# Reordering the three partial products inside whole matmul units of an encoder step on one Trainium2 core

## The chip, the cores and the metric

One core of one Trainium2 chip. The metric is the device time of one execution in microseconds, as the median of the runs; the profile is one further execution, recorded by the hardware profiler. Engines are TensorE (PE; its weight loads are PEld), VectorE (DVE), ScalarE (ACT), GpSimd (POOL) and SyncE (SP), which issues most DMAs.

## What is computed

A two-layer encoder trunk for 512 prompt positions and 64 sample positions, which share all weights. Cut to what matters:

```python
for i in range(2):
    h = x + 0.5 * rmsnorm(swiglu(rmsnorm(x), f1_up, f1_down))     # FFN 1, 1024 -> 2 x 2816 -> 1024
    u = rmsnorm(h)
    branch inputs, gates = split(u @ w_in)                         # 1024 -> 2816 + 4096
    y_n = branch_n(...) @ w_branch[n]                              # conv, gated recurrence, two attentions
    m = sum_n sigmoid(gate_n) * y_n
    h = h + rmsnorm(m @ w_out)
    h = h + 0.5 * rmsnorm(swiglu(rmsnorm(h), f2_up, f2_down))     # FFN 2
    h = h + rmsnorm((p[i] @ ple_w) * sigmoid(rmsnorm(h) @ ple_gate_w))
```

All data are float32. The kernel works with activations turned, features on the 128 partitions and all T = 576 positions along the free axis.

## The kernel before, in words

**Three products.** Each float32 operand is held as a rounded part and a remainder (`whi`/`wlo` for weights, `u_hi`/`u_lo`, `s_hi`/`s_lo`, `o_hi`/`o_lo`, `m_split[..0]`/`m_split[..1]` for inputs). A product is rounded weights by rounded inputs, plus rounded weights by input remainders, plus weight remainders by rounded inputs, all added up in PSUM.

**Units.** A unit is one load of weights of 128 x 1024 (128 output features, up to 8 input tiles of 128), 512 KB by one DMA into one of RAW = 4 slots of `wraw`. A unit yields 128 output features for all 576 positions, in two halves of 288. So a whole unit is 8 tiles x 3 products x 2 halves = 48 matmuls. The third unit of each down-projection output has 6 tiles. A layer has 222 units: 44 + 24 for FFN 1, 22 projections, 40 of gates and branches, 8 of the output projection, 44 + 24 for FFN 2, 2 + 8 for the per-layer embedding (PLE).

**How a unit's weights come.** SyncE loads into slot i % 4 when `w_split` says that the slot's last user is split (`load_unit`, L505). ScalarE rounds `wraw` into `whi[i % 2]` when unit i - 2 is done (`act_round`, L499 to L503) and counts `w_rounded`. GpSimd then makes `wlo[i % 2]` (L1830 to L1832) and counts `w_split`. TensorE waits on `w_split` at the start of the unit (`split_ready`, L541).

**How TensorE walks a unit.** `products` (L527 to L539) goes by input tile k; per tile it runs all three products, six matmuls. `wait_k` waits ahead of each tile, in the units whose inputs are still being made: the first after a norm, and the first output-projection unit. Line L536 is the matmul of all units.

**Norm and first unit.** After a norm's sum (`pe_norm_y` L572, `pe_norm_h` L581) TensorE broadcasts the factors into PSUM (`pe_broadcast` L565) and runs filler matmuls (`keep_clock` L549): 14 calls ahead of FFN 1, 6 calls ahead of the others. Then VectorE makes the eight normed tiles `uf[k]` (L742), ScalarE rounds each to `u_hi[k]` (L659, signal `u_high`), and the remainder `u_lo[k]` is made by GpSimd for k = 1, 2, 4, 5, 6 and by VectorE for k = 0, 3, 7 (`low`, L736; signals `u_ready_pool` and `u_ready`). `u_tile_ready` (L589) waits for the remainder of tile k. There are four such first units in a layer: FFN 1, projections, FFN 2, PLE gate.

**Gated sum and output projection.** `dve_gates` (L1577) makes the gated sum tile by tile: it adds up `msum`, casts it into `m_split[:, m, 0]` (L1596), makes the remainder (L1597) and counts `m_ready`. `pe_out` (L1546) runs the eight output-projection units; the first waits for `m_ready` tile by tile.

**Partial units.** Where a unit is laid between steps of a recurrence or an attention, `unit_part` (L809) runs two or three tiles of it at a time through `products`; the branch products in `pe_gates` (L1523) use `products` too.

Of the kernel before, what the change touches and what calls it, by code (L numbers as in the profile page):

```python
# [33 lines left out]
HT = T // 2  # L34
# [10 lines left out]
KD = D // 128  # L45
# [15 lines left out]
U_UP, U_DOWN = 2 * KF, 3 * KD  # L61
U_FFN = U_UP + U_DOWN
U0_FFN1 = 0
U0_PROJ = U_FFN
U0_GATE = U0_PROJ + NPROJ
# [7 lines left out]
SPLIT = 2  # L73
# [15 lines left out]
def trunk(nc, a, o):  # L89
    n_consts = [0]  # L90
    n_placed = [0]
    with ExitStack() as ctx:
# [26 lines left out]
        whi = keep("whi", [SPLIT, 1024], F32R)  # L119
# [407 lines left out]
        def products(pe, part, x_hi, x_lo, ks, k_off, p, start, stop, wait_k=None):  # L527

            ins = None
            for n, k in enumerate(ks):  # L530
                if wait_k is not None:
                    wait_k(k)
                w = slice(128 * (k_off + n), 128 * (k_off + n) + 128)
                for c, (wt, x) in enumerate(((whi, x_hi), (whi, x_lo), (wlo, x_hi))):
                    for f in range(2):
                        ins = pe.matmul(ps[:, 2 * p + f, 0:HT], wt[:, part, w], x[:, k, HT * f:HT * f + HT],  # L536
                                        start=start and n == 0 and c == 0, stop=stop and n == len(ks) - 1 and c == 2,
                                        skip_group_check=True)
            return ins  # L539

        def split_ready(pe, i):  # L541
            pe.wait_ge(w_split, i + 1 + RAW)

# [45 lines left out]
        def u_tile_ready(pe, n):  # L589

            def wait(k):
                if k in LO_POOL:
                    pe.wait_ge(u_ready_pool, len(LO_POOL) * (n // 2) + LO_POOL.index(k) + 1)
                else:
                    pe.wait_ge(u_ready, len(LO_DVE) * (n // 2) + LO_DVE.index(k) + 1)
            return wait

        def pe_ffn(pe, f, u0):
            if f == 0:
                keep_clock(pe, 14)  # L600
                pe_norm_y(pe, N_F1PRE)
            else:
                pe_norm_h(pe, N_F2PRE)
            with pe.Fori(0, KF // 2) as it:
                for q in range(4):
                    i = it * 4 + (u0 + q)
                    split_ready(pe, i)

                    pe.wait_ge(up_mul, it * 2 + (f * KF + q // 2 + 1))

                    products(pe, (u0 + q) % SPLIT, u_hi, u_lo, range(KD), 0, q, True, True,
                             wait_k=u_tile_ready(pe, 4 * f + N_F1PRE) if q == 0 else None).then_inc(unit_done, 1)
            with pe.Fori(0, 2) as it:
                for m in range(4):
                    for q, (k0, k1) in enumerate(DOWN_K):
                        i = it * 12 + (u0 + U_UP + 3 * m + q)
                        split_ready(pe, i)
                        if q == 0:

                            pe.wait_ge(y_ready, it * 4 + (m + 1 + y_before[4 * f + N_F1POST]))  # L620
                        if m == 0 and q != 1:

                            pe.wait_ge(s_ready, f * KF + 2 + (KF - 1 if q == 0 else KF))
                        products(pe, (u0 + U_UP + 3 * m + q) % SPLIT, s_hi, s_lo, range(k0, k1), 0, m, q == 0, q == 2).then_inc(unit_done, 1)
            if f:
                pe_turn_p(pe)
            pe.wait_ge(y_ready, 4 + y_before[4 * f + N_F1POST] + 5)
            pe_norm_y(pe, 4 * f + N_F1POST)
# [186 lines left out]

        def pe_proj_free(pe, t):

            split_ready(pe, U0_PROJ + t)
            if t >= 2:
                pe.wait_ge(proj_out, t - 1)  # L820

        def pe_proj(pe, t):
            i = U0_PROJ + t
            pe_proj_free(pe, t)
            products(pe, i % SPLIT, u_hi, u_lo, range(KD), 0, t % 2, True, True,
                     wait_k=u_tile_ready(pe, N_MPRE) if t == 0 else None).then_inc(unit_done, 1)

        def pe_proj_part(pe, t, j, parts):
            if j == 0:
                pe_proj_free(pe, t)  # L830
            unit_part(pe, U0_PROJ + t, j, t % 2, parts)

# [253 lines left out]

        def pe_gate_free(pe, g):

            split_ready(pe, U0_GATE + g)
            if g == 0:  # L1090
                pe.wait_ge(proj_out, NPROJ)
            elif g < GATES_CONV:
                pe.wait_ge(gate_out, g - 1)
            else:
                pe.wait_ge(gate_out, g)

        def pe_kept_gate(pe, g):
            pe_gate_free(pe, g)
            products(pe, (U0_GATE + g) % SPLIT, u_hi, u_lo, range(KD), 0, g % 2, True, True).then_inc(unit_done, 1)

        def pe_gate_part(pe, n, last, step, parts):

            g, j = n + step // len(parts), step % len(parts)
            if g < last:
                if j == 0:
                    pe_gate_free(pe, g)
                unit_part(pe, U0_GATE + g, j, 0, parts)

# [414 lines left out]
        def pe_gates(pe):  # L1523
            with pe.Fori(0, 2) as it:
                for m in range(4):
                    u0 = U0_PAIR + 3 * m
                    i = it * 12 + u0
                    split_ready(pe, i)
                    if m == 0:
                        pe.wait_ge(gate_out, 2 * KD)  # L1530
                    for n in range(NB):
                        if m == 0:
                            pe.wait_ge(o_ready, 2 * n + 2)
                        if n >= 2:

                            pe.wait_ge(sig_done, it * 8 + (2 * m + n - 1))
                        ins = products(pe, u0 % SPLIT, o_hi, o_lo, (2 * n, 2 * n + 1), 2 * n, n, True, True)
                    ins.then_inc(unit_done, 1)
                    for n in (2, 3):
                        split_ready(pe, i + (n - 1))  # L1540
                        pe.wait_ge(yb_out, it * 16 + (4 * m + n - 1))
                        products(pe, (u0 + n - 1) % SPLIT, u_hi, u_lo, range(KD), 0, n, True, True).then_inc(unit_done, 1)

                    pe.wait_ge(yb_out, it * 16 + (4 * m + 4))

        def pe_out(pe):  # L1546
            for m in range(KD):
                i = U0_OUT + m
                split_ready(pe, i)
                if m >= 4:  # L1550
                    pe.wait_ge(y_ready, y_before[N_MPOST] + m + 1)

                products(pe, i % SPLIT, m_split[:, :, 0, :], m_split[:, :, 1, :], range(KD), 0, m % 4, True, True,
                         wait_k=(lambda k: pe.wait_ge(m_ready, k + 1)) if m == 0 else None).then_inc(unit_done, 1)
            pe.wait_ge(y_ready, 4 + y_before[N_MPOST] + 5)
            pe_norm_y(pe, N_MPOST)

# [129 lines left out]
        def pe_ple(pe):  # L1687
            for q in range(2):
                i = U0_PLEW + q
                split_ready(pe, i)  # L1690
                pe.wait_ge(p_ready, 2)
                for m in range(4):

                    j = 4 * q + m
                    if j >= 3:
                        pe.wait_ge(e_out, j - 2)
                    for kk in range(2):
                        for c, (wt, x) in enumerate(((whi, p_hi), (whi, p_lo), (wlo, p_hi))):
                            for f in range(2):
                                ins = pe.matmul(ps[:, 2 * (j % 3) + f, 0:HT], wt[:, i % SPLIT, 512 * kk + 128 * m:512 * kk + 128 * m + 128],  # L1700
                                                x[:, kk, HT * f:HT * f + HT], start=kk == 0 and c == 0, stop=kk == 1 and c == 2, skip_group_check=True)
                    ins.then_inc(e_made, 1)
                pe.wait_ge(e_made, 4 * q + 4)
                pe.sem_inc(unit_done, 1)
            pe.wait_ge(e_out, KD)
            pe_norm_h(pe, N_PPRE)
            for m in range(KD):
                i = U0_PLEG + m
                split_ready(pe, i)
                if m >= 4:  # L1710
                    pe.wait_ge(ple_sig, m - 3)
                products(pe, i % SPLIT, u_hi, u_lo, range(KD), 0, m % 4, True, True,
                         wait_k=u_tile_ready(pe, N_PPRE) if m == 0 else None).then_inc(unit_done, 1)
            pe.wait_ge(ple_sig, 5)
            pe_norm_y(pe, N_PPOST)

# [253 lines left out]
```

## Time and profile before

| | |
|---|---|
| median of 3 runs | 3511.64 us (3510.53 to 3516.72) |
| profiled execution, its own time | 3519.2 us |
| span of its instructions | 3517.5 us |
| TensorE matmuls busy | 3266.0 us, 23523 matmuls |
| weight loads busy | 3105.9 us |
| VectorE, ScalarE, GpSimd busy | 1386.8, 1096.2, 1206.1 us |
| mean granted clock of TensorE | 0.957 |
| moved by DMA | 236.25 MB, mean 67 GB/s |

The busy time of an engine is the time in which at least one of its instructions runs. A matmul's row lasts about 0.29 us since matmuls overlap; what a matmul costs is the distance from one start to the next. A wait is told as "engine, line waited for <- engine and line that released it". A granted clock of 1.00 is 2.4 GHz, 0.50 is 1.2 GHz.

### The profile page before, as it was taken

How to read it: one execution, taken by the hardware profiler on the slowest of the kernel's cores; microseconds unless marked ns; L12 is line 12 of the kernel's file. 1: busy time of each engine (PE TensorE's matmuls, PEld its weight loads, DVE VectorE, ACT ScalarE, POOL GpSimd, SP SyncE). 2: the span in 40 equal slices, each digit the busy share in tenths (PEclk: the TensorE clock that was granted, in tenths of full speed). 3: DMA queues.
4: the chain of work that ended last, by engine and by line, in shares of the span. 5: the costliest groups of instructions: out<-in, count | busy, mean ns of one | idle time of the engine just before them, and what ended most of it. 6: DMA issues, size and time to landing. Idle time of an engine off the chain costs nothing. (4 is left out here: it accounts for less than half of the span.)

```text
span 3517.5 us, 56480 instructions
## 1 busy us (share of the span) xinstructions
PE 3266.0 (93%) x23523; PEld 3105.9 (88%) x23523; DVE 1386.8 (39%) x1793; ACT 1096.2 (31%) x1518; POOL 1206.1 (34%) x538
## 2 busy tenths in 40 slices
PE   8999998877999999999889999988789999999997
PEld 7999986776699899999789999867676998999987
DVE  4222144784444323312333321548844433332133
ACT  3332231124533333323233322311255333333232
POOL 4333442131134433344333334411211434333442
PEclk9999998998999999999899999989899999999988
DMA  3222211121122122232022222111210221222211
GB/s 95 83 81 82 83 57 49 37 77 51 31 66 78 55 83 78 82 89 75 13 85 82 79 84 83 54 41 44 67 53 26 78 82 56 82 79 87 83 59 40
DMA packets 455963, 236.25 MB, mean 67 GB/s; under 512 B 18630, under 2 KB 454150, under 8 KB 455814
## 3 DMA queue, kind: packets, MB, share of 16 engines
q1 hardware_dynamic: 445792, 227.05, 22.1%
q10 hardware_dynamic: 10022, 7.15, 0.7%
q8 instruction: 102, 1.67, 0.2%
q14 instruction: 47, 0.39, 0.0%
HBM read 228.53 MB, written 5.63 MB: 67 GB/s over the span
## 5 line engine op out<-in xcount | busy, mean ns | idle before, releaser
L1832 POOL TENSOR_TENSOR wlo<-wraw,whi 128x1024 fp32r<-128x1024 f32 x432 | 1076.3, 2492 | 2122.3 <-ACT whi L503 2122.3
L536 PE MATMUL ps<-u_hi,whi 128*128 128x288 f32 x4800 | 1062.2, 302 | 36.3 <-ACT ybr L1565 11.8
L536 PE MATMUL ps<-u_lo,whi 128*128 128x288 f32 x4800 | 1038.2, 297 | 0.0
L536 PE MATMUL ps<-u_hi,wlo 128*128 128x288 f32 x4800 | 1037.2, 297 | 0.0
L536 PEld LDWEIGHTS ps<-u_hi,whi 128*128 128x128 f32 x4800 | 778.4, 191 | 73.3 <-issue 33.0
L536 PEld LDWEIGHTS ps<-u_lo,whi 128*128 128x128 f32 x4800 | 779.5, 190 | 0.0
L536 PEld LDWEIGHTS ps<-u_hi,wlo 128*128 128x128 f32 x4800 | 778.0, 190 | 0.0
L503 ACT ACTIVATE whi<-wraw 128x1024 fp32r<-128x1024 f32 x432 | 456.9, 1058 | 959.0 <-PE ps L536 958.5
L783 DVE TENSOR_TENSOR sq<-sq,ps 128x576 f32<-128x576 f32 x88 | 66.4, 754 | 751.0 <-PE ps L536 751.0
L536 PE MATMUL ps<-s_hi,wlo 128*128 128x288 f32 x1408 | 302.7, 296 | 0.0
L536 PE MATMUL ps<-s_lo,whi 128*128 128x288 f32 x1408 | 302.7, 296 | 0.0
L536 PE MATMUL ps<-s_hi,whi 128*128 128x288 f32 x1408 | 302.6, 296 | 0.0
L720 DVE TENSOR_TENSOR sqsum<-sqsum,sq 128x576 f32<-128x576 f32 x70 | 102.0, 1458 | 506.5 <-ACT sq L638 504.3
L787 DVE TENSOR_TENSOR s_lo<-sq,s_hi 128x576 f32 x88 | 241.5, 2745 | 10.9
L536 PEld LDWEIGHTS ps<-s_hi,whi 128*128 128x128 f32 x1408 | 226.5, 189 | 0.0
L536 PEld LDWEIGHTS ps<-s_hi,wlo 128*128 128x128 f32 x1408 | 226.5, 189 | 0.0
L536 PEld LDWEIGHTS ps<-s_lo,whi 128*128 128x128 f32 x1408 | 226.3, 189 | 0.0
L1167 DVE SCALAR_TENSOR_TENSOR yc<-zc,taps,yc 128x606 f32<-128x606 f32 x120 | 134.4, 1122 | 4.2
L503 ACT ACT_TABLE_LOAD x44 | 56.5, 1283 | 232.4 <-PE ps L536 232.4
L553 PE MATMUL ps<-ident,ones 128*128 128x128 f32 x528 | 88.3, 333 | 22.9 <-issue 18.7
L553 PEld LDWEIGHTS ps<-ident,ones 128*128 128x128 f32 x528 | 82.7, 244 | 23.3 <-issue 23.2
L854 ACT ACTIVATE proj<-ps 128x576 f32<-128x576 f32 x28 | 18.3, 652 | 233.6 <-PE ps L536 233.6
(277 smaller groups left out, 2985.3 us busy)
## 6 DMA issues: line engine op xcount, KB each, us to landing
wraw<-in_ffn_up SPq DMA_DIRECT2D x176, 512.0 KB, 3.8
wraw<-in_w_in SPq DMA_DIRECT2D x104, 512.0 KB, 3.8
wraw<-in_ffn_down SPq DMA_DIRECT2D x64, 512.0 KB, 3.8
wraw<-in_ffn_down SPq DMA_DIRECT2D x32, 384.0 KB, 3.3
wraw<-in_w_out SPq DMA_DIRECT2D x16, 512.0 KB, 3.8
wraw<-in_ple_gate_w SPq DMA_DIRECT2D x16, 512.0 KB, 3.8
wraw<-in_w_branch SPq DMA_DIRECT2D x16, 256.0 KB, 2.7
xtok<-in_x_prompt SPq DMA_DIRECT2D x4, 512.0 KB, 6.6
```

The costliest lines, as they stand in the source:

```text
L503: act.activation(whi[:, i % SPLIT, :], wraw[:, i % RAW, :], ACT.Copy).then_inc(w_rounded, 1)
L536: ins = pe.matmul(ps[:, 2 * p + f, 0:HT], wt[:, part, w], x[:, k, HT * f:HT * f + HT], start=start and n == 0 and c == 0, stop=stop and n ...
L553: pe.matmul(ps[:, 1, 0:128], ones[:], ident[:], start=True, stop=True)
L720: dve.tensor_tensor(sqsum[:], sqsum[:], sq[:, k % 2, :], ALU.add).then_inc(sq_added, 1)
L783: dve.tensor_tensor(halves(x), halves(x), pair(2 * q + 1), ALU.mult).then_inc(up_mul, 1)
L787: dve.tensor_tensor(s_lo[:, bass.ds(it * 2 + q, 1), :].rearrange("p a n -> p (a n)"), x, s_hi[:, bass.ds(it * 2 + q, 1), :].rearrange("p a ...
L854: ins = act.activation(x, y_, ACT.Copy, scale=HD ** -0.5 if t in (BQ_, BQ_ + 1) else 1.0)
L1167: ins = dve.scalar_tensor_tensor(out=yc[:, c, :], in0=zc[:, c, w:w + YW], scalar=wc, in1=yc[:, c, :], op0=ALU.mult, op1=ALU.add)
L1832: pool.tensor_tensor(wlo[:, i % SPLIT, :], wraw[:, i % RAW, :], whi[:, i % SPLIT, :], ALU.subtract).then_inc(w_split, 1)
```

## The change

`products` stays for partial units. Whole units (FFN up and down, whole projections, kept gates, the gates in `pe_gates`, output projection, PLE gate) go through a new function `unit`. It runs one product over all tiles of the unit, then the next: rounded weights by rounded inputs, rounded weights by input remainders, weight remainders by rounded inputs. The wait for `w_split` moves to the start of the last third; at the start of the unit stands a wait for `w_rounded`. In the first units after a norm the first third waits for `u_high` tile by tile and the second third for the remainders as before. In the first output-projection unit the first third waits for `m_ready`. Partial units call `split_ready` themselves, ahead of their first part.

```diff
+        def unit(pe, i, part, x_hi, x_lo, ks, p, start, stop, wait_hi=None, wait_k=None):
+            pe.wait_ge(w_rounded, i + 1)
+            ins = None
+            for c, (wt, x) in enumerate(((whi, x_hi), (whi, x_lo), (wlo, x_hi))):
+                if c == 2:
+                    split_ready(pe, i)
+                for n, k in enumerate(ks):
+                    if c == 0 and wait_hi is not None:
+                        wait_hi(k)
+                    if c == 1 and wait_k is not None:
+                        wait_k(k)
+                    w = slice(128 * n, 128 * n + 128)
+                    for f in range(2):
+                        ins = pe.matmul(ps[:, 2 * p + f, 0:HT], wt[:, part, w], x[:, k, HT * f:HT * f + HT],
+                                        start=start and n == 0 and c == 0, stop=stop and n == len(ks) - 1 and c == 2,
+                                        skip_group_check=True)
+            return ins
...
+        def u_high_ready(pe, n):
+            return lambda k: pe.wait_ge(u_high, 8 * (n // 2) + k + 1)
...
-                    split_ready(pe, i)
                     pe.wait_ge(up_mul, it * 2 + (f * KF + q // 2 + 1))
-                    products(pe, (u0 + q) % SPLIT, u_hi, u_lo, range(KD), 0, q, True, True,
-                             wait_k=u_tile_ready(pe, 4 * f + N_F1PRE) if q == 0 else None).then_inc(unit_done, 1)
+                    unit(pe, i, (u0 + q) % SPLIT, u_hi, u_lo, range(KD), q, True, True,
+                         wait_hi=u_high_ready(pe, 4 * f + N_F1PRE) if q == 0 else None,
+                         wait_k=u_tile_ready(pe, 4 * f + N_F1PRE) if q == 0 else None).then_inc(unit_done, 1)
...
-                split_ready(pe, i)
                 if m >= 4:
                     pe.wait_ge(y_ready, y_before[N_MPOST] + m + 1)
-                products(pe, i % SPLIT, m_split[:, :, 0, :], m_split[:, :, 1, :], range(KD), 0, m % 4, True, True,
-                         wait_k=(lambda k: pe.wait_ge(m_ready, k + 1)) if m == 0 else None).then_inc(unit_done, 1)
+                unit(pe, i, i % SPLIT, m_split[:, :, 0, :], m_split[:, :, 1, :], range(KD), m % 4, True, True,
+                     wait_hi=(lambda k: pe.wait_ge(m_ready, k + 1)) if m == 0 else None).then_inc(unit_done, 1)
```

The down-projection units, the whole projections, the kept gates, the two gate units in `pe_gates` and the PLE gate units are changed in the same way; counted over both layers, 388 units go through `unit`.

## Rows read from the trace of the kernel before

**Rows 1.** The page, busy time of each engine.
```profile
PE 3266.0 (93%) x23523; PEld 3105.9 (88%) x23523; DVE 1386.8 (39%) x1793; ACT 1096.2 (31%) x1518; POOL 1206.1 (34%) x538
```

**Rows 2.** TensorE's waits: waiter <- releaser, us in total, times, longest us.
```profile
PE ps L536 <- POOL u_lo L736: 11.6, 28, 0.6
...
PE ps L536 <- DVE u_lo L736: 5.7, 6, 1.1
...
PE ps L536 <- POOL wlo L1832: 1.5, 2, 0.8
...
PE ps L536 <- DVE m_split L1597: 0.3, 2, 0.2
```

**Rows 3.** FFN 1's up-projections: stretch, us; busy PE, PEld, DVE, ACT, POOL; clock, DMA, GB/s.
```profile
52.00:320.00 268.00, 268.00 (x2012) 268.00 (x2011) 83.15 (x63) 85.07 (x85) 104.20 (x42) 1.00 0.28 81
```

**Rows 4.** Timeline of FFN 2's first unit: start, us, engine, line, operation, xcount [idle <- releaser].
```profile
1209.20 1.56 PE L553 MATMUL ps<-ident,ones 128*128 128x128 f32 x12
1211.87 0.51 PE L536 MATMUL ps<-u_hi,whi 128*128 128x288 f32 x2 [1.11 <-DVE u_lo L736]
...
1219.66 0.53 PE L536 MATMUL ps<-u_hi,whi 128*128 128x288 f32 x2 [0.32 <-POOL u_lo L736]
1220.03 0.42 PE L536 MATMUL ps<-u_lo,whi 128*128 128x288 f32 x2
...
1221.35 0.43 PE L536 MATMUL ps<-u_hi,whi 128*128 128x288 f32 x2
...
1210.25 1.41 ACT L659 ACTIVATE u_hi<-uf 128x576 fp32r<-128x576 f32 x2 [3.42 <-DVE uf L742]
1212.49 2.13 ACT L659 ACTIVATE u_hi<-uf 128x576 fp32r<-128x576 f32 x3 [0.82 <-DVE uf L742]
1216.04 2.13 ACT L659 ACTIVATE u_hi<-uf 128x576 fp32r<-128x576 f32 x3 [1.42 <-DVE uf L742]
...
1218.21 2.02 DVE L736 TENSOR_TENSOR u_lo<-uf,u_hi 128x576 fp32r<-128x576 f32 x1 [0.75 <-ACT u_hi L659]
...
1216.80 2.80 POOL L736 TENSOR_TENSOR u_lo<-uf,u_hi 128x576 fp32r<-128x576 f32 x2 [0.23 <-ACT u_hi L659]
```

**Rows 5.** Timeline of the first output-projection unit, first layer.
```profile
1133.53 0.70 PE L536 MATMUL ps<-m_split,whi 128*128 128x288 f32 x4
...
1136.08 2.53 DVE L1596 CAST m_split<-msum 128x576 fp32r<-128x576 f32 x1
...
1138.64 0.76 DVE L1597 TENSOR_TENSOR m_split<-msum,m_split 128x576 fp32r<-128x576 f32 x1
...
1139.45 0.79 PE L536 MATMUL ps<-m_split,whi 128*128 128x288 f32 x4 [0.15 <-DVE m_split L1597]
...
1140.35 0.70 PE L536 MATMUL ps<-m_split,whi 128*128 128x288 f32 x4
```

**Rows 6.** TensorE's clock: stretch, us, busy PE, clock, DMA, GB/s; below, the sums at 1186.85.
```profile
551.60:554.60 3.00, 0.01 (x1) 0.94 0.35 67
...
556.40:561.40 5.00, 4.97 (x16) 0.54 0.48 105
...
1186.20:1189.10 2.90, 2.06 (x17) 1.00 0.24 73
...
1190.60:1195.90 5.30, 5.26 (x18) 0.50 0.35 99
...
1211.90:1221.40 9.50, 7.79 (x49) 1.00 0.00 0
...
970.00:974.10 4.10, 3.81 (x16) 0.50 0.00 0
...
1186.85 1.27 PE L559 MATMUL ps<-ones,sqsum 128*128 128x1 f32 x10 [0.64 <-DVE sqsum L720]
```

**Rows 7.** Timeline at half clock: two matmuls in each row, first branch product.
```profile
971.87 0.69 PE L536 MATMUL ps<-o_hi,whi 128*128 128x288 f32 x2
972.35 0.69 PE L536 MATMUL ps<-o_lo,whi 128*128 128x288 f32 x2
```

More of the change, by code:

```diff
@@ L623, in pe_ffn @@
                             pe.wait_ge(s_ready, f * KF + 2 + (KF - 1 if q == 0 else KF))
-                        products(pe, (u0 + U_UP + 3 * m + q) % SPLIT, s_hi, s_lo, range(k0, k1), 0, m, q == 0, q == 2).then_inc(unit_done, 1)
+                        unit(pe, i, (u0 + U_UP + 3 * m + q) % SPLIT, s_hi, s_lo, range(k0, k1), m, q == 0, q == 2).then_inc(unit_done, 1)
             if f:
@@ L816, in pe_proj_free @@
         def pe_proj_free(pe, t):
-            split_ready(pe, U0_PROJ + t)
             if t >= 2:
@@ L824, in pe_proj @@
             pe_proj_free(pe, t)
-            products(pe, i % SPLIT, u_hi, u_lo, range(KD), 0, t % 2, True, True,
-                     wait_k=u_tile_ready(pe, N_MPRE) if t == 0 else None).then_inc(unit_done, 1)
+            unit(pe, i, i % SPLIT, u_hi, u_lo, range(KD), t % 2, True, True,
+                 wait_hi=u_high_ready(pe, N_MPRE) if t == 0 else None, wait_k=u_tile_ready(pe, N_MPRE) if t == 0 else None).then_inc(unit_done, 1)
         def pe_proj_part(pe, t, j, parts):
             if j == 0:
+                split_ready(pe, U0_PROJ + t)
                 pe_proj_free(pe, t)
@@ L1087, in pe_gate_free @@
         def pe_gate_free(pe, g):
-            split_ready(pe, U0_GATE + g)
             if g == 0:
@@ L1098, in pe_kept_gate @@
             pe_gate_free(pe, g)
-            products(pe, (U0_GATE + g) % SPLIT, u_hi, u_lo, range(KD), 0, g % 2, True, True).then_inc(unit_done, 1)
+            unit(pe, U0_GATE + g, (U0_GATE + g) % SPLIT, u_hi, u_lo, range(KD), g % 2, True, True).then_inc(unit_done, 1)
         def pe_gate_part(pe, n, last, step, parts):
@@ L1105, in pe_gate_part @@
                 if j == 0:
+                    split_ready(pe, U0_GATE + g)
                     pe_gate_free(pe, g)
@@ L1539, in pe_gates @@
                     for n in (2, 3):
-                        split_ready(pe, i + (n - 1))
                         pe.wait_ge(yb_out, it * 16 + (4 * m + n - 1))
-                        products(pe, (u0 + n - 1) % SPLIT, u_hi, u_lo, range(KD), 0, n, True, True).then_inc(unit_done, 1)
+                        unit(pe, i + (n - 1), (u0 + n - 1) % SPLIT, u_hi, u_lo, range(KD), n, True, True).then_inc(unit_done, 1)
                     pe.wait_ge(yb_out, it * 16 + (4 * m + 4))
@@ L1548, in pe_out @@
                 i = U0_OUT + m
-                split_ready(pe, i)
                 if m >= 4:
                     pe.wait_ge(y_ready, y_before[N_MPOST] + m + 1)
-                products(pe, i % SPLIT, m_split[:, :, 0, :], m_split[:, :, 1, :], range(KD), 0, m % 4, True, True,
-                         wait_k=(lambda k: pe.wait_ge(m_ready, k + 1)) if m == 0 else None).then_inc(unit_done, 1)
+                unit(pe, i, i % SPLIT, m_split[:, :, 0, :], m_split[:, :, 1, :], range(KD), m % 4, True, True,
+                     wait_hi=(lambda k: pe.wait_ge(m_ready, k + 1)) if m == 0 else None).then_inc(unit_done, 1)
             pe.wait_ge(y_ready, 4 + y_before[N_MPOST] + 5)
@@ L1708, in pe_ple @@
                 i = U0_PLEG + m
-                split_ready(pe, i)
                 if m >= 4:
                     pe.wait_ge(ple_sig, m - 3)
-                products(pe, i % SPLIT, u_hi, u_lo, range(KD), 0, m % 4, True, True,
-                         wait_k=u_tile_ready(pe, N_PPRE) if m == 0 else None).then_inc(unit_done, 1)
+                unit(pe, i, i % SPLIT, u_hi, u_lo, range(KD), m % 4, True, True,
+                     wait_hi=u_high_ready(pe, N_PPRE) if m == 0 else None, wait_k=u_tile_ready(pe, N_PPRE) if m == 0 else None).then_inc(unit_done, 1)
             pe.wait_ge(ple_sig, 5)
```

## The prediction, made before the change was run

> **What bounds the kernel now.** I read the page's busy line first: TensorE is busy for 93% of the span, the next engine for 39% [rows 1]. Then the waits of TensorE, to see whether it ever stands for the thing that the change moves. The remainder of the weights (wlo, made by GpSimd) is waited for twice, 1.5 us in all; the remainders of the inputs (u_lo) 34 times, 11.6 + 5.7 = 17.3 us; the last split tile of the gated sum (m_split) twice, 0.3 us [rows 2]. Then a stretch with no wait at all, for the price of one matmul: 2012 in 268.0 us at clock 1.00, 133.2 ns each, over some forty unit boundaries, each with its waits [rows 3]. A whole unit is 8 tiles x 3 products x 2 halves = 48 matmuls, 6.4 us; a third of it is 2.13 us. So the kernel is a long row of 6.4 us units without gaps, and the change can move time only where a unit has to wait in the middle: at its inputs, or at a clock that has fallen.
>
> **Inside a run of units: nothing.** The changed unit has the same 48 matmuls, with as many weight loads. It has one more satisfied wait (w_split, ahead of the last third). Satisfied waits stand at each unit boundary of the stretch and don't show: 133.2 ns a matmul is the same as inside a unit [rows 3]. I take 0. The upper bound is what the first pair after a real wait costs: 0.37 us to the next pair (1219.66 to 1220.03) against 0.27, so 0.10 us [rows 4]; with 388 whole units that is 39 us, but nothing in the stretch looks like it. Below nothing is excluded: no matmul is taken out.
>
> **The waits for wlo: a gain of 1.5 us.** Both [rows 2] lie in the third unit after a mixer's norm, where ScalarE rounded late. Rounded weights now suffice to start; wlo is needed 4.3 us later. Both waits go. Elsewhere the earlier start is worth nothing, because TensorE doesn't wait.
>
> **The first unit after a norm: a loss of 1.5 us, eight times.** There are four such units a layer (FFN 1, projections, FFN 2, PLE gate). Take the one at 1210 us [rows 4]. ScalarE makes the eight u_hi tiles in three bursts, the last three from 1216.04 for 2.13 us: u_hi[7] is there at 1218.17. The last remainders follow: GpSimd ends u_lo[6] at 1219.60 and VectorE u_lo[7] at 1220.23. Before, TensorE goes tile by tile behind the remainders: it starts at 1211.87, does tile 6 from 1219.66, tile 7 directly behind, and starts the next unit at 1221.35. By the time the last tile is there, only 12 matmuls are left. After the change the first third waits for u_hi[7]: 1218.17 + 0.06 for the wait (1219.60 to 1219.66 is the same) + 0.37 for the restarted pair = 1218.60. The second third needs u_lo[6] at 1218.60 + 6 x 0.267 = 1220.2 and u_lo[7] at 1220.5, both there, and ends 1220.73. The last third ends 1222.86. That is 1.51 us later than 1221.35, though the unit began a micro-second earlier and the 17.3 us of waits for u_lo are gone from the list; in their place stands a wait for u_hi, by ScalarE, in the first third. The other seven have the same pattern (the first unit of each layer's FFN 1 starts later, behind a longer filler, but it too ends by its last tiles). 8 x 1.51 = **12.1 us**. Behind each of them comes work of TensorE or work that waits for it, so it all counts.
>
> **The first output-projection unit: a loss of 3.8 us, twice.** Its input is m_split. Before, it starts at 1133.53 while VectorE still makes tile 7: a 2.53 us cast from 1136.08, then the remainder, until 1139.40 [rows 5]. Tiles 0 to 6 cover that nearly exactly: tile 7 starts at 1139.45 and the next unit at 1140.35. After the change m_ready[k] is waited for in the first third, and it counts only when both halves are made. The first third has 7 tiles, 14 x 0.133 = 1.9 us, so TensorE stands from 1135.4 to 1139.45, and then owes 34 matmuls: 0.36 for the restarted pair and 32 x 0.133, to 1144.08, 3.73 us later. Twice, **7.5 us**. Here the cover was the rest of the same unit, and the change puts it behind the wait.
>
> **The clock: a loss of about 16 us.** From 551.6 TensorE stands for 4.8 us (the first row of the clock's group covers 3.0 of them), the clock falls to half (1.2 GHz), and after the work is back it stays at half for 5.0 us; from 1190.6 for 5.3, from 970.3 for 3.8 [rows 6]. At half clock a pair of these matmuls takes 0.48 us (971.87 to 972.35) [rows 7] against 0.267, so each micro-second at half loses 0.445. That prices one fall at 1.7 to 2.4 us; I take 2.1 (4.7 us). The two output-projection units now hold a gap of 4.0 us, like the one of 4.8 us: I count both. Whether the six norm units with the short filler fall too (it ends at 1210.8) is the open question. In their first third TensorE now has 2.13 us of matmuls spread over the 7.4 us from 1211.2 to 1218.6, with gaps up to some 2 us. Nearest rows: from 1211.90 to 1221.40, 7.79 us of 9.50 busy, no fall [rows 6]; from 1186.20 to 1189.10, 2.06 of 2.90 us busy, most of it filler of 128 columns and sums of one column, the longest gap 0.64 us [rows 6]: the clock fell at its end. A third of the time with matmuls is thinner than that, so I count all six. The two FFN 1 units have filler into the middle of the stretch; bounds 0 and 2.4, I take 0. 8 x 2.1 = **16.8 us**; bounds 0 and 24.
>
> The Trainium skill ("TensorE: Matmul & The Clock Gate", section "Why this matters for your kernels") asks for no idle gaps over about 3 us between bursts. By it the two output-projection units lose the clock and the norm units, with gaps up to 2 us, keep it; this case's fall at 1189.1 behind a gap of 0.64 us speaks against taking it as the only condition. It is the first rival below.
>
> **Sum.** -1.5 + 12.1 + 7.5 + 16.8 = +34.9 us. The profiled execution took 3519.2 us, which makes 3554.1; it stands 7.6 us above the median of the runs, 3511.64, so I set the forecast at 3511.64 + 34.9, about **3546 us** (+1.0%).
>
> **Rivals.**
> 1. The norm units keep the clock; only the two long gaps lose it. For: the gaps of 2 us at most, and nothing fell from 1211.90 to 1221.40. Against: the fall at 1189.1. -1.5 + 12.1 + 7.5 + 2 x 2.1 = 22.3, 3534 us. Chance 0.25.
> 2. The extra wait in the middle of a unit holds back the weight load behind it and opens the row each time: 388 x 0.10 = 39 us more, 3585 us. Against it are forty boundaries without a trace. It decides if the pair behind a satisfied w_split wait comes more than 0.27 us after the one before. Chance 0.05.
> 3. Faster. The waits for u_lo (17.3) and wlo (1.5) go and nothing comes in their place: 18.8 us less, 3493 us. This needs u_hi[7] to come 4.5 us or more before the old unit's end, so that the two thirds behind it fit in; it comes 3.2 us before (1218.17 against 1221.35). It would decide if ScalarE's tiles weren't paced by VectorE's; they are, by its three bursts. Even with it the output projection takes back 7.5. Chance 0.03.
> 4. The losses fall into slack, and the change does little: the projections after the mixer's norm feed chains of VectorE that TensorE waits for later. But those chains begin with the late unit's own output, so they shift with it. Within 0.2%: chance 0.04.
> The forecast itself has 0.63.
>
> **Range and chances.** Low end: 3511.6 + 18.1, no fall anywhere, is 3530; rival 1 is inside. High end: all ten units at 2.4 us and the norm losses as they are, 3511.6 + 18.1 + 24, 3554, with 6 for what the shifted phases do to the other clock falls: 3560. I take 3528 to 3560; rivals 2, 3 and 4 are out. A measurement here can tell about 0.2%, 7 us. Slower by more: 0.63 + 0.25 + 0.05 = 0.93; the same 0.04; faster 0.03.
>
> **What the changed profile would show.** In the list of waits u_lo is nearly gone, wlo is gone, u_hi (ScalarE) stands with 20 us or more over the eight norm units, and m_split with about 8 us in two waits. The unit after 1210 us ends 12.6 us after the first u_hi starts, if the clock holds (11.1 before). The granted clock shows 0.50 behind the first output unit, and in the norm units or not, which decides between the forecast and rival 1. A stretch inside FFN 1's up-projections still has 2012 matmuls in 268 us; if it has fewer, rival 2 holds. I am wrong if the end of those first units doesn't move, or if TensorE's matmuls in an undisturbed stretch change their pace.

## The result, and the profile after

The changed kernel takes 3543.15 us (median of 4 runs, 3539.37 to 3543.6) against 3511.09 for the kernel before (4 runs, 3502.98 to 3516.72): ratio 1.0091, 95% interval 1.007 to 1.0112. It is slower, by 32 us. The profiled execution took 3543.09 us, with a span of 3541.4; that is 23.9 us more than the span before.

The page's busy line hardly moves, and that is right: the same 23523 matmuls run.

```profile
span 3541.4 us, 56640 instructions
PE 3275.2 (92%) x23523; PEld 3112.9 (88%) x23523; DVE 1382.2 (39%) x1793; ACT 1095.8 (31%) x1518; POOL 1205.2 (34%) x538
```

The list of TensorE's waits answers to [rows 2]. L555 is the matmul of the new `unit`, L680 ScalarE's rounding of u_hi, L1616 the remainder of m_split.

```profile
PE ps L555 <- ACT u_hi L680: 20.9, 31, 1.6
...
PE ps L555 <- DVE m_split L1616: 7.7, 2, 3.8
```

The waits for u_lo (17.3 us) and for wlo (1.5 us) are gone. In their place stand 20.9 us for u_hi and 7.7 us for m_split. By this list alone the change would cost 28.6 - 19.1 = 9.5 us, m_split's 0.3 of before counted too. What it can't show is how much work each wait leaves behind it, and at what clock that work runs. (By its matmuls of L555 the trace holds 384 units that go through `unit`, not 388; no term of the forecast hangs on that.)

A stretch of FFN 1's up-projections, against [rows 3] (columns: stretch, us, busy PE, clock, DMA, GB/s):

```profile
55.00:323.00 268.00, 268.00 (x2012) 1.00 0.28 80
```

2012 matmuls in 268 us, as before. Inside a run of units whose inputs are ready nothing has changed.

FFN 2's first unit, against [rows 4], in the timeline:

```profile
1221.19 1.17 PE L555 MATMUL ps<-u_hi,whi 128*128 128x288 f32 x4 [0.32 <-ACT u_hi L680]
1223.33 2.30 PE L555 MATMUL ps<-u_hi,whi 128*128 128x288 f32 x6 [0.97 <-ACT u_hi L680]
1226.88 2.30 PE L555 MATMUL ps<-u_hi,whi 128*128 128x288 f32 x6 [1.25 <-ACT u_hi L680]
1228.98 2.88 PE L555 MATMUL ps<-u_lo,whi 128*128 128x288 f32 x16
1231.70 2.30 PE L555 MATMUL ps<-u_hi,wlo 128*128 128x288 f32 x16
1233.83 2.30 PE L555 MATMUL ps<-u_hi,whi 128*128 128x288 f32 x16
```

The first rounded input starts at 1220.37. TensorE starts 0.82 us later, where it took 1.62 before, waits in the first third, and then still has two thirds to do. The granted clock is at half from 1223.5 to 1230.3, so the second third, which begins in that stretch, takes 2.72 us instead of 2.13. The next unit starts 13.46 us after that first input, against 11.10 before. The first output-projection unit, against [rows 5]:

```profile
1137.34 2.03 PE L555 MATMUL ps<-m_split,whi 128*128 128x288 f32 x14
1143.21 4.69 PE L555 MATMUL ps<-m_split,whi 128*128 128x288 f32 x18 [3.84 <-DVE m_split L1616]
1147.69 2.60 PE L555 MATMUL ps<-m_split,wlo 128*128 128x288 f32 x16
1150.13 1.10 PE L555 MATMUL ps<-m_split,whi 128*128 128x288 f32 x7
```

Seven tiles, a stand of 3.84 us, then 34 matmuls, the first of them at half clock: 12.79 us from start to the next unit, against 6.82.

**Where the time went.** Measured in the same way over the whole run (first rounded input to next unit, before and after), the eight units after a norm lengthened by 3.0, 3.6, 2.4 and 2.9 us in the first layer and 2.5, 3.0, 2.4 and 2.9 in the second, 22.5 us in all; the two output-projection units by 5.97 us each, 11.9. That is 34.4 us in ten units. The stretch from FFN 2's second unit to the PLE gate's first input (67 units, the embedding and two norms) got shorter by 6.2 us in each layer (459.2 to 453.0), 12.4 us. Its place is one row, 80 sums over tokens of 64 columns, of the kernel before:

```profile
1660.86 14.90 PE L559 MATMUL ps<-ones,sq 128*128 128x64 f32 x80 [0.74 <-ACT e L1725]
```

and of the changed one:

```profile
1674.00 9.14 PE L578 MATMUL ps<-ones,sq 128*128 128x64 f32 x80 [0.74 <-ACT e L1743]
```

Before, they ran at half clock, in both layers; after, at full. The rest (-1.6 in the start, the mixers and the output projections together, +3.5 in the PLE gates, their norms and the end) is small pieces, at most 3.1 us each, which I didn't take apart. Hence two questions for experiments: is it the ten units, and in them how much is the order and how much the clock; and is the time given back by the sums an effect of the clock alone?

### The profile page after: what moved, and what is told of

Same layout as the page of the kernel before. It is cut to its first block and busy times, and to the rows that moved or that the text cites. A ratio compares the mean times of both kernels' runs of the same rounds, so it can differ in the third digit from the quotient of the medians.

```text
span 3541.4 us, 56640 instructions
## 1 busy us (share of the span) xinstructions
PE 3275.2 (92%) x23523; PEld 3112.9 (88%) x23523; DVE 1382.2 (39%) x1793; ACT 1095.8 (31%) x1518; POOL 1205.2 (34%) x538
## 5 line engine op out<-in xcount | busy, mean ns | idle before, releaser
L555 PE MATMUL ps<-u_hi,whi 128*128 128x288 f32 x4352 | 661.0, 304 | 35.5 <-ACT u_hi L680 20.9
L555 PEld LDWEIGHTS ps<-u_hi,whi 128*128 128x128 f32 x4352 | 613.6, 194 | 55.2 <-ACT u_hi L680 32.4
L555 PE MATMUL ps<-u_lo,whi 128*128 128x288 f32 x4352 | 633.8, 299 | 0.0
L555 PE MATMUL ps<-u_hi,wlo 128*128 128x288 f32 x4352 | 624.8, 296 | 0.0
L555 PEld LDWEIGHTS ps<-u_lo,whi 128*128 128x128 f32 x4352 | 605.6, 192 | 0.0
L555 PEld LDWEIGHTS ps<-u_hi,wlo 128*128 128x128 f32 x4352 | 595.8, 189 | 0.0
L555 PE MATMUL ps<-s_hi,whi 128*128 128x288 f32 x1408 | 203.4, 296 | 0.0
L555 PE MATMUL ps<-s_hi,wlo 128*128 128x288 f32 x1408 | 203.4, 296 | 0.0
L555 PE MATMUL ps<-s_lo,whi 128*128 128x288 f32 x1408 | 203.4, 296 | 0.0
L555 PEld LDWEIGHTS ps<-s_hi,wlo 128*128 128x128 f32 x1408 | 193.2, 189 | 0.0
L555 PEld LDWEIGHTS ps<-s_lo,whi 128*128 128x128 f32 x1408 | 193.2, 189 | 0.0
L555 PEld LDWEIGHTS ps<-s_hi,whi 128*128 128x128 f32 x1408 | 193.2, 189 | 0.0
L536 PE MATMUL ps<-u_hi,whi 128*128 128x288 f32 x448 | 112.7, 334 | 3.4 <-ACT proj L1139 3.4
L572 PEld LDWEIGHTS ps<-ident,ones 128*128 128x128 f32 x528 | 78.5, 234 | 24.6 <-issue 24.4
```

The costliest lines, as they stand in the source:

```text
L572: pe.matmul(ps[:, 1, 0:128], ones[:], ident[:], start=True, stop=True)
```

## The experiments

Eight kernels ran. For each the ratio is to the kernel before on the same chip, with its 95% interval.

**1. The output projection alone goes back.**

```diff
-                unit(pe, i, i % SPLIT, m_split[:, :, 0, :], m_split[:, :, 1, :], range(KD), m % 4, True, True,
-                     wait_hi=(lambda k: pe.wait_ge(m_ready, k + 1)) if m == 0 else None).then_inc(unit_done, 1)
+                if m == 0:
+                    split_ready(pe, i)
+                    products(pe, i % SPLIT, m_split[:, :, 0, :], m_split[:, :, 1, :], range(KD), 0, m % 4, True, True,
+                             wait_k=lambda k: pe.wait_ge(m_ready, k + 1)).then_inc(unit_done, 1)
+                else:
+                    unit(pe, i, i % SPLIT, m_split[:, :, 0, :], m_split[:, :, 1, :], range(KD), m % 4, True, True).then_inc(unit_done, 1)
```

> Only the first output-projection unit of each layer goes tile by tile again; all else as in the changed kernel. If the loss sits in the ten units whose inputs come late: that unit takes 6.8 us from its first matmul to the next unit's, instead of 12.8, with no half clock in it, and the run is 12 us shorter than the changed kernel, near 3531 us, +0.6% against the kernel before. If the extra wait in the middle of every unit costs: the unit comes back the same, but the units elsewhere keep a pace above 6.40 us. If the clock alone made the loss there: the unit keeps the 3.7 us and only some 2 go.

3530.4 us, ratio 1.0044 (1.0029 to 1.0059). The two units take 6.82 us again, without half clock, as expected: 11.9 us. The ratio falls from 1.0091 to 1.0044, 16 us, with intervals of some 7 and 5 us on either side; the 12 fit in. Seven of the eight norm units stay at 13.6 to 14.8. The eighth, the first layer's FFN 1, began 3.96 us after its first rounded input, behind the long filler, with the clock back at full, and took 12.60 us without a fall. The profile held a surprise in FFN 2 of the first layer:

```profile
1232.00:1500.00 268.00, 268.00 (x2063) 1.00 0.29 86
```

That is 129.9 ns a matmul at the same granted clock of 1.00, over some 400 us; the second layer is back at the usual pace. I come back to it below.

**2. The first units after the norms alone go back.** `first_back` waits for w_split and calls `products` with `u_tile_ready`, as the kernel before does; it is called for q == 0 in FFN up, t == 0 in the projections and m == 0 in the PLE gate. Since q == 0 is every fourth unit of an FFN's up-projections, 48 of the 384 units go back with it, an eighth and not the sixth that the expectation names; 40 of them had their inputs ready anyway.

```diff
+        def first_back(pe, i, part, p, n):
+            split_ready(pe, i)
+            products(pe, part, u_hi, u_lo, range(KD), 0, p, True, True, wait_k=u_tile_ready(pe, n)).then_inc(unit_done, 1)
...
+                    if q == 0:
+                        first_back(pe, i, (u0 + q) % SPLIT, q, 4 * f + N_F1PRE)
+                    else:
+                        unit(pe, i, (u0 + q) % SPLIT, u_hi, u_lo, range(KD), q, True, True).then_inc(unit_done, 1)
```

> Only the first unit after each of the eight norms goes tile by tile behind the remainders again (in FFN up, every fourth unit with it, since the loop body is one). If the loss sits in the late inputs: the eight units take 11.1 us from the first rounded input to the next unit, instead of 13.5 to 14.7, with no fall of the clock, and the run is 22 us shorter than the changed kernel, near 3521 us, +0.3% against before. If the clock fell in those units for another reason than their thin first third, half clock is still seen in them. If the middle wait costs, a sixth of the units is rid of it and the rest keeps it.

3519.39 us, ratio 1.0005 (0.999 to 1.002). The eight units are at 11.08 to 11.13 us with no half clock in any, exactly as expected; the two output-projection units at 12.76 and 12.82. But the kernel should have been 10 us slower than before and is within 4 us of it (3516.07). The stretch ahead of the PLE gate accounts for it in the profile: 454.1 us in both layers, against 459.2 before. Here too the sums run in 9.14 us.

**3. Both go back.** Both edits together: 50 of the 384 units go tile by tile, and the other 334, all with ready inputs, still run by thirds.

> Both of the above at once: what is left of the change is the order and the middle wait in all units whose inputs are ready. If that is free: 3510 us, 1.5 us less than before for the two waits for the weights' remainders, within 0.2% of before. If the wait in the middle opens the row of matmuls by 0.1 us each: some 30 us more than before, and fewer than 2012 matmuls in 268 us of FFN 1. If the order itself were faster or slower in the array (other use of the weights, of the input reads), the pace of 133.3 ns a matmul changes in either direction.

3514.77 us against 3516.07, ratio 0.9993 (0.9983 to 1.0003). What is left of the change is free as far as 12 runs against 31 can show, to some 3.5 us: the reordering and the wait in the middle cost nothing in the units that keep them, where 0.1 us each would be 33 us. The 1.5 us of the two waits fit in. The stretch of FFN 1 again:

```profile
52.00:320.00 268.00, 268.00 (x2012) 1.00 0.28 82
```

In this kernel, where the late units are as before, the sums ahead of the PLE gate are back at half clock (14.95 and 14.93 us), and the stretch at 459.2 us.

**4. Filler in the gaps.** The changed kernel with `ones` by `ident` matmuls into a free PSUM bank, in six of the ten late units.

```diff
+                        for _ in range(fill.get(k, 0)):
+                            pe.matmul(ps[:, bank, 0:128], ones[:], ident[:], start=True, stop=True)
                         wait_hi(k)
...
+                 fill={2: 4, 5: 6, 6: 1, 7: 1}).then_inc(unit_done, 1)
...
+                     wait_hi=(lambda k: pe.wait_ge(m_ready, k + 1)) if m == 0 else None, fill={7: 14}, bank=2).then_inc(unit_done, 1)
```

> The changed kernel with filler matmuls in the gaps of the first third of six late units (projections, PLE gate: 4, 6, 1 and 1 ahead of tiles 2, 5, 6, 7; output projection: 14 ahead of tile 7); FFN 1 and FFN 2 stay without. If the fall of the clock is a cost of its own beside the order: no half clock in the six units, 12.6 us instead of 14 in the four after a norm and 10.6 instead of 12.8 in the two of the output projection, while the four FFN units keep their half clock and 13.5 to 14.1 us; about 10 us less than the changed kernel, near 3533 us. If the clock falls for another reason, the six units stay as they are or get longer by the filler.

Ratio 1.0013 (0.9991 to 1.0035), 3518.03 us. In the order of time: the output projection's unit, FFN 2's (no filler) and the PLE gate's, in the first layer:

```profile
1132.37:1142.88 10.51, 9.78 (x78) 1.00 0.30 86
1211.87:1225.38 13.51, 10.77 (x53) 0.75 0.01 1
1678.41:1691.01 12.60, 11.45 (x77) 1.00 0.01 1
```

The filled units hold clock 1.00 and take 10.51, 10.52 and 12.59 to 12.60 us. Of the four unfilled FFN units three fall as before and take 13.5 us; the fourth, the second layer's FFN 1, began only 3.65 us after its first input, behind the long filler, and took 12.61 without a fall. So each loss has two parts that can be read apart: after a norm 12.60 - 11.10 = 1.50 us for the order, and 0.9 to 2.1 for the clock; in the output projection 3.69 and 2.28. The expectation for the units was met, the one for the time was not. The kernel was to lie 10 us below the changed one, near 3533; it lies 27 us below by the two ratios, and 21.7 by the spans of the profiles. The six filled units gave 10.9 of the 21.7 and the two FFN 1 units 1.5; the other 9 are pieces of 0.9 to 2.9 us in the start, the norms and a mixer, none of them touched by the edit. Why these moved is open.

**5. Another order in the late units.** Products with the rounded input run as soon as it is there; the product with the remainder follows two tiles behind. The output projection's first unit goes tile by tile. In FFN up the lagged order, too, is taken in every fourth unit; all other whole units stay as in the change.

```diff
+        def first_lag(pe, i, part, p, n):
+            split_ready(pe, i)
...
+            for k in range(KD + 2):
+                if k < KD:
+                    wait_hi(k)
+                    pair_of(whi, u_hi, k, k == 0, False)
+                    pair_of(wlo, u_hi, k, False, False)
+                if k >= 2:
+                    wait_k(k - 2)
+                    ins = pair_of(whi, u_lo, k - 2, False, k - 2 == KD - 1)
+            ins.then_inc(unit_done, 1)
```

> The changed kernel with another order in the ten late units: the output projection tile by tile as before; in the first unit after a norm each tile's two products with the rounded input (by rounded weights and by weight remainders) run as soon as the rounded input is there, and the product with the input remainder follows two tiles behind. If what counts is how many matmuls are left when the last input arrives: two are left behind u_lo[7] (9.98 us after the first rounded input starts), so the next unit starts at 10.4 us instead of 11.1 before and 13.5 to 14.7 in the changed kernel, with no fall of the clock; 8 x 0.7 + 1.5 = 7 us less than the kernel before, -0.2%. If the clock falls here too (gaps before tiles 2 and 5 remain), 11.5 us or more. On top, either sign: the 80 sums ahead of the PLE gate run at full or half clock (9.1 or 14.9 us, twice).

3498.2 us, ratio 0.9955 (0.9939 to 0.9971): it lies below both kernels, but only in part by its order. All eight units take 10.42 to 10.44 us, none falls. The end of FFN 2's:

```profile
1211.59 0.53 PE L627 MATMUL ps<-u_hi,whi 128*128 128x288 f32 x2 [0.91 <-ACT u_hi L701]
...
1214.48 1.15 PE L627 MATMUL ps<-u_lo,whi 128*128 128x288 f32 x4 [0.24 <-POOL u_lo L778]
1215.47 0.81 PE L555 MATMUL ps<-u_hi,whi 128*128 128x288 f32 x5
```

Four matmuls are left behind GpSimd's last remainder, u_lo[6], where the kernel before has twelve and the change, counted from the last rounded input, thirty-four. These units give 8 x 0.68 = 5.4 us and the waits for wlo 1.5. The sums at full clock (9.14 us, twice; the stretch 454.2 us in the second layer, 459.2 before) give about 10. Together 17, against 15.9 between the medians. (The profiled execution, at 3480.14 us, lies lower still: two of its stages ran at the faster pace of the last section.)

**6 and 7. Wider token sums.** One number, in the lagged kernel and in the kernel before.

```diff
-        SAME = 64
+        SAME = 96
```

> The same, with the token sums of the norms 96 instead of 64 equal columns wide, so that TensorE does more in the same waits. If the 80 sums of a norm fall to half clock because they are thin: in all six such norms they take 9 to 10.5 us and none 14.9, and the time is that of the lagged order with full-clock sums, about 3500 us. If they fall for where they lie in time alone, 14.9 us or more still occurs in the norm ahead of the PLE gate.

> The kernel before with 96 instead of 64 equal columns in the token sums, nothing else. If the sums ahead of the PLE gate are at half clock for being thin: 9 to 10.5 us instead of 14.9, twice, so 9 to 12 us less than before, 0.3%; and the 12 us that the changed kernel took less in that stage are this and not its order. If not, the sums stay at 14.9 and the time is that of before or, with the longer matmuls, up to 5 us more.

The kernel before with wider sums: 3504.82 us, ratio 0.9972 (0.9963 to 0.9981). The sums ahead of the PLE gate:

```profile
1659.05 9.17 PE L559 MATMUL ps<-ones,sq 128*128 128x96 f32 x80 [0.74 <-ACT e L1725]
```

9.17 us instead of 14.90, in both layers, and the stretch is at 452.4 us. 96 columns cost as much as 64 at full clock (9.07 against 9.04 elsewhere), and here the clock held. The time falls by 10 us with no other change. The single runs fit this. The kernel before, with 64 columns, drifts from run to run on this chip: from 3504.0 us at a mean granted clock of 0.963 to 3519.2 at 0.957. The ten runs of the widened one all have 0.961 to 0.963 and 3500.7 to 3507.1 us. So the kernel before has executions without the loss, too; that it was its sums that held in them is likely, but they weren't profiled.

The lagged kernel gains nothing more by the widening (3501.94 us, ratio 0.9952, 0.9933 to 0.997), since its sums were at full clock already. Between these two widened kernels the order alone is left: 0.9952 / 0.9972 = 0.9980, 7 us, where 5.4 + 1.5 = 6.9 were to come. That is no more than the two intervals together (some 7 us), so the time alone doesn't prove it; the eight units at 10.42 to 10.43 us against 11.09 to 11.13 do.

**8. The changed kernel with wider sums.** The same edit.

> The changed kernel with 96 instead of 64 equal columns in the token sums, nothing else. It is to be read against the kernel before with the same widening, whose sums all ran at full clock (3504.8 us, 0.9972 of the kernel before). If the ten late units cost 34.4 us, the waits for wlo give 1.5 back, and the rest of the gap to the measured change came from the sums ahead of the PLE gate: those sums stay near 9.2 us here, the units stay at 13.5 to 14.7 and 12.8 us, and the time is 3504.8 + 33 = 3538 us, 1.0066 of the kernel before. If the sums weren't the reason, this kernel keeps its distance to the kernel before and lies at 3543 us or above, or the late units become shorter.

3541.1 us, ratio 1.0075 (1.0053 to 1.0097). The sums take 9.17 us, the late units 13.5 to 14.5 and 12.8. Against the widened kernel before, the change now costs 1.0075 / 0.9972 = 1.0103, 36 us, with some 8 us of interval either way: the 34.4 of the ten units less 1.5 fit in. But 1.0075 lies between the two values that the expectation set apart (1.0066, and 1.0091 for an unchanged distance), and its interval holds both, so the time doesn't decide between them; nor does it tell 36 us from the 32 of the unwidened pair. What decides is the stage: 453.0 us in both layers here, the same as in the changed kernel with 64 columns, while the same edit took the kernel before from 459.2 to 452.4.

## Why the prediction was right

The forecast was 3546 us, +34.9, with a chance of 0.93 for slower; measured were 3543.15 and +32.1 (24.6 to 39.3 by the interval). The mechanism was right. That the number came within 3 us is partly luck, since a term was missing and the clock's was wrongly spread. Step by step:

- **Inside a run of units, 0.** Right: 2012 matmuls in 268 us, and experiment 3 shows the remainder of the change as free. Rival 2, the middle wait that opens the row, is dead.
- **The waits for wlo, -1.5.** Right: the line is gone. Too small to be told in the time.
- **The first unit after a norm, 8 x 1.51.** Right in place and size: 1.50 us where filler keeps the clock (experiment 4). What decides is how much of the unit is left when its last input arrives. An earlier start buys nothing: the unit of experiment 1 that began 3.1 us later than the others, without any added filler, took the same 12.60 us as the filled ones.
- **The output projection, 2 x 3.73.** Right: 3.69 with filler, and 12 us back in experiment 1.
- **The clock, 8 x 2.1 = 16.8.** Right in kind, and nearly in sum: what the ten units lost beyond the measured 8 x 1.50 and 2 x 3.69 is 34.4 - 12.0 - 7.4 = 15.0 us. The split was off. I took 0 for the two FFN 1 units with the long filler; they fell too, for 1.5 and 1.0 us. The six others lost 0.9 to 2.1, 1.35 in the mean, where I took 2.1 for each, because part of the half clock lay in the first third, where TensorE waits anyway (in FFN 2's first unit from 1223.5 to 1229.0). The output-projection units lost 2.28 each. (A row behind this term is read a little high: after 556.4 the clock was at half for 4.6 us and not 5.0; the 4.7 us taken don't change by it.)
- **Rival 1, no fall in the norm units**, was wrong in every one of eight. The longest stand in them is 1.6 us. The Trainium skill's rule ("TensorE: Matmul & The Clock Gate", section "Why this matters for your kernels"), no idle gaps over about 3 us, is met there and doesn't hold the clock. The row that I set against it, the fall at 1189.1 behind a gap of 0.64 us [rows 6], was the better guide: there, too, no long gap stood before the fall.
- **Rival 3, faster**, needed the last rounded input 4.7 us before the old end (0.43 for the wait and the restarted pair and 4.26 for two thirds; the prediction says 4.5), and it comes 3.2 before. The lagged order of experiment 5 gets what was real in it, 0.68 us a unit, by leaving little behind the last input.
- **What the sum lacked** is a term of the other sign: -12.4 us in the sums ahead of the PLE gate, whose clock was low before and wasn't after. I named "what the shifted phases do to the other clock falls" with 6 us in the high end only, so a loss; it came as a gain. In the profiled pair it is the main reason why the spans differ by 23.9 and not by some 36. The medians differ by 32, so there it can't have weighed as much; the kernel before drifts by 15 us from run to run (experiment 7), and its profiled execution, 3519.2 us, was longer than any of the four runs behind its median.

What stays open is why the 80 sums fall in one kernel and not in another. In seven kernels with 64 columns, two layers each, they fell in both layers of the kernel before and of experiment 3, in one layer of experiment 1, and in no layer of the changed kernel and of experiments 2 and 4; nor did they in experiment 5's two. With 96 columns they held six times of six; only the two of the kernel before had fallen with 64, so it is these two, and the narrower spread of its ten runs, that show an effect of the width. No run tells whether the earlier falls in the late units are what shifts them.

## What to carry to other kernels

Order the partial products of a unit by when their inputs arrive, and count what is left behind the last arrival; the start of the unit doesn't matter if its end hangs on that arrival. Turn the loop inside out only for units whose inputs are all there. There it cost nothing that these runs can show, and it gained nothing that they can show either. And before a small difference is put down to an edit, compare stage by stage the stretches that the edit doesn't touch: here an untouched row of sums took back 12.4 of the 34.4 us in the profiled pair.

## What was unexpected of the hardware

In the changed kernel TensorE's clock fell in eight first units of eight, in or just behind the first third, with stands of at most 1.6 us. The sixteen matmuls of that third, 2.13 us at full clock, were spread over 7.8 us in six of the units, and over 4.9 and 6.1 us in FFN 1's two. With filler in the gaps it held, six times of six (four of these units and both of the output projection's). Sums of 64 columns, 80 in a row, ran at either clock (9.1 or 14.9 us); with 96 columns they took 9.17 us and held the full clock in all three kernels that had them.

A dense row of the same matmuls has two paces at the same granted clock of 1.00. The usual is 268.0 / 2012 = 133.2 ns. In experiment 1 and in experiment 5 it was 129.9 ns for whole stages:

```profile
1230.00:1498.00 268.00, 268.00 (x2064) 1.00 0.29 85
70.00:338.00 268.00, 268.00 (x2013) 1.00 0.28 81
```

These are FFN 2 and FFN 1 of the first layer in experiment 5, in the same execution. A stage at the faster pace is 10 us shorter (444.0 us against 454.2 in the second layer). It is seen three times in the traces and may be part of why, beside the drift of the clock, single runs of one kernel lie up to 33 us apart (3489.42 to 3522.61 for the kernel before). What sets the pace wasn't tried.
